# One stage of a hybrid layer with mixture of experts: the masking of the RWKV core's k products moves from VectorE to ScalarE and GpSimd

## What is computed

```python
def step(state, inp):
    r_t, w_t, k_t, v_t, kk_t, a_t = inp
    sa = jnp.einsum('bhij,bhj->bhi', state, -kk_t)
    state = (state * w_t[:, :, None, :]
             + sa[..., :, None] * (kk_t * a_t)[..., None, :]
             + v_t[..., :, None] * k_t[..., None, :])
    return state, jnp.einsum('bhij,bhj->bhi', state, r_t)
```

## Time and profile before

| | |
|---|---|
| median of 3 runs | 1987.44 us (1983.1 to 1991.18) |
| the profiled execution's own time | 1987.7 us |
| its span | 1986.1 us |
| TensorE matmul busy | 1891.4 us (95%) |
| TensorE weight loads busy | 1511.3 us (76%) |
| VectorE busy | 1577.8 us (79%) |
| ScalarE busy | 1212.9 us (61%) |
| GpSimd busy | 440.2 us (22%) |

### The profile page before, as it was taken

One profiled execution on the slowest core, in us unless ns is written; L12 is line 12 of the kernel. 1 busy time (PEld: TensorE's weight loads), 2 busy tenths in 40 slices (PEclk: granted clock), 3 DMA queues, 4 the chain that ended last, 5 costly groups with the idle time before them and its releaser, 6 DMA issues.

```text
span 1986.1 us, 27242 instructions
## 1 busy us (share of the span) xinstructions
PE 1891.4 (95%) x9408; PEld 1511.3 (76%) x9408; DVE 1577.8 (79%) x1614; ACT 1212.9 (61%) x1246; POOL 440.2 (22%) x385
## 2 busy tenths in 40 slices
PE   7999988999999889899999999999999999999997
PEld 5766655787767677788888888888888888888884
DVE  5763344775385569889999999999999999999996
ACT  5545564425374312467777777777777777777773
POOL 4535543001061421331111111111111111111110
PEclk9999998999999879799999999999999999999998
DMA  7535442414101124789999999999999999999993
GB/s 207 166 114 183 138 144 75 167 43 117 32 1 33 22 91 147 265 312 382 396 399 389 398 390 391 394 388 394 384 393 383 395 395 380 398 387 394 383 377 127
DMA packets 176497, 525.06 MB, mean 264 GB/s; under 512 B 30434, under 2 KB 47922, under 8 KB 176434
## 3 DMA queue, kind: packets, MB, share of 16 engines
q1 hardware_dynamic: 152722, 457.48, 60.2%
q0 software_dynamic: 21632, 66.74, 11.7%
q10 hardware_dynamic: 2080, 0.01, 0.1%
HBM read 499.06 MB, written 25.12 MB: 264 GB/s over the span
## 4 chain that ended last, share of the span: by engine, by line
PE 57%; DVE 2%; issue 0%; POOLq 0%; POOL 0%; DVEq 0%
PE banks L3436 53%; PE banks L3424 3%; PE banks L3430 1%; PE banks L3500 0%; DVE expert_weights L3774 0%; DVE x_tokens L3770 0%; PE banks L3521 0%; DVE weights_lo L3570 0%; DVE x_tokens L3781 0%; DVE x_tokens L3653 0%; PE banks L3557 0%; PE banks L3491 0%; DVE rows_lo L3600 0%; DVE member L3633 0%; DVE route_work L3675 0%
## 5 line engine op out<-in xcount | busy, mean ns | idle before, releaser
L3570 DVE TENSOR_TENSOR weights_lo<-expert_weights,weights_hi 128x2048 fp32r<-128x2048 f32 x384 | 877.1, 2288 | 65.6 <-ACT weights_hi L3810 61.3
L3810 ACT ACTIVATE weights_hi<-expert_weights 128x2048 fp32r<-128x2048 f32 x384 | 739.0, 1926 | 264.6 <-PE banks L3436 259.1
L3436 PE MATMUL banks<-weights_hi,rows_hi 128*128 128x512 f32 x1024 | 319.2, 393 | 0.0
L3436 PE MATMUL banks<-weights_hi,rows_lo 128*128 128x512 f32 x1024 | 315.5, 389 | 0.0
L3436 PE MATMUL banks<-weights_lo,rows_hi 128*128 128x512 f32 x1024 | 273.8, 389 | 0.0
L3436 PEld LDWEIGHTS banks<-weights_hi,rows_hi 128*128 128x128 f32 x1024 | 189.7, 188 | 44.9 <-issue 7.0
L3436 PEld LDWEIGHTS banks<-weights_hi,rows_lo 128*128 128x128 f32 x1024 | 192.2, 188 | 40.5
L3436 PEld LDWEIGHTS banks<-weights_lo,rows_hi 128*128 128x128 f32 x1024 | 192.2, 188 | 39.9
L3436 PE MATMUL banks<-weights_hi,u_hi 128*128 128x512 f32 x512 | 161.8, 397 | 0.0
L3436 PE MATMUL banks<-weights_hi,u_lo 128*128 128x512 f32 x512 | 158.8, 391 | 0.0
L3436 PE MATMUL banks<-weights_lo,u_hi 128*128 128x512 f32 x512 | 137.7, 391 | 0.0
(11 more groups left out here) (608 smaller groups left out, 2831.9 us busy)
## 6 DMA issues: line engine op xcount, KB each, us to landing
expert_weights<-in_exp_w SPq DMA_DIRECT2D x384, 1024.0 KB, 10.3
enter_rows<-in_ada_w POOLq DMA_DIRECT2D x24, 1024.0 KB, 5.7
w_in_landing<-in_w_in SPq DMA_DIRECT2D x16, 384.0 KB, 3.3
second_landing<-in_w_in SPq DMA_DIRECT2D x12, 512.0 KB, 4.0
x_tokens<-in_x SPq DMA_DIRECT2D x8, 512.0 KB, 7.1
w_in_landing<-in_w_in SPq DMA_DIRECT2D x8, 512.0 KB, 3.7
rwkv_room<-in_w_o SPq DMA_DIRECT2D x8, 512.0 KB, 7.5
w_in_landing<-in_w_in SPq DMA_DIRECT2D x12, 256.0 KB, 3.7
```

The lines of the kernel that those rows point to most:

```text
L3436: last = nc.tensor.matmul(c.banks[:, bank + n, :], left[:, 2 * q + kk, :], right[:, q, kk * FF + n * 512:kk * FF + (n + 1) * 512], start=s ...
L3570: nc.vector.tensor_tensor(w_lo[:, ch % SPLIT, :], c.raw[:, ch % RAW if place is None else place, :], w_hi[:, ch % SPLIT, :], ALU.subtract) ...
L3810: nc.scalar.activation(w_hi[:, ch % SPLIT, :], c.raw[:, ch % RAW if place is None else place, :], ACT.Copy).then_inc(hi_ready.sem, 1)
```

## The change

ScalarE copies both kinds of a unit's k products from PSUM into kv_mat as they are (copy_k), and GpSimd then zeroes what the mask zeroed, in place, with two affine selects. VectorE's mask function goes. kv_mat gets three slots. TensorE's k products of unit i wait for ScalarE's copy of unit i - 3, since that frees the banks; its mv units wait for GpSimd's selects. On ScalarE the copies of units 0 to 2 stand ahead of the 12 row copies, those of units 3 to 7 behind the square root of the latent sums, and the copies of banks 6 and 7 for tiles 0 and 1 stand behind copy_k(4) and copy_k(6).

```diff
--- before.py
+++ after.py
@@ -2632,7 +2632,8 @@
     X0 = work(TT, RH, P)
     bc_mat = work(TT, RH, P)
     staged = free(2, RH, P)
-    kv_mat = Carve(X0.rearrange("p t h s -> p (t h s)"))(2, 2, 4, P)
+    KV = 3
+    kv_mat = Carve(X0.rearrange("p t h s -> p (t h s)"))(KV, 2, 4, P)
     scale = Carve(staged.rearrange("p a h s -> p (a h s)"))
     scale_next, rhs = scale(TT - 1, RP, P), scale(RW)
     state = free(TT - 1, RP, P)
@@ -2649,6 +2650,7 @@
     rows_turned, rows_copied = own("token_rows_turned"), own("token_rows_copied")
     latent_sums, latent_roots, latent_ready = own("latent_sums"), own("latent_roots"), own("latent_ready")
     k_ready, k_masked, mv_done, mv_copied = own("k_products_ready"), own("k_products_masked"), own("mv_done"), own("mv_copied")
+    k_copied = own("k_products_copied")
     y_ready, y_copied, x_ready, x_taken = own("y_ready"), own("y_copied"), own("x_ready"), own("x_taken")
     z_ready, z_copied, j_ready, j_copied = own("z_ready"), own("z_copied"), own("join_ready"), own("join_copied")
     scales, rhs_ready, rhs_added, u_ready, u_copied = (own("scales_ready"), own("rhs_ready"), own("rhs_added"), own("u_ready"),
@@ -2722,6 +2724,15 @@
                 nc.gpsimd.memset(XTB[:].rearrange("p a b -> p (a b)")[:, 0:S * S:S + 1], 1.0).then_inc(cleared.sem, 1)
                 nc.gpsimd.memset(inverse, 0.0).then_inc(x_cleared.sem, 1)
 
+                for i in range(units):
+
+                    pool.wait_ge(k_copied.sem, i + 1)
+                    for kind, compare in enumerate((ALU.is_gt, ALU.is_ge)):
+                        place = kv_mat[:, i % KV, kind]
+                        last = nc.gpsimd.affine_select(out=place, in_=place, compare_op=compare, fill=0.0, base=0,
+                                                       pattern=[[0, 4], [1, P]], channel_multiplier=-1)
+                    last.then_inc(k_masked.sem, 1)
+
                 pool.wait_ge(solved.sem, 1)
                 for t in range(TT - 1):
                     along = lambda x, at: x[:, :, at:at + 1].broadcast_to([P, RP, P])
@@ -2779,7 +2790,7 @@
                             pe.wait_ge(b_masked.sem, 5 + i)
                         else:
 
-                            pe.wait_ge(k_masked.sem, i - 2)
+                            pe.wait_ge(k_copied.sem, i - 2)
                         for h, f, j, n in heads_of(q):
                             both = ar[rows_of(j), f, t, :, :].rearrange("p k s -> p (k s)")
                             last = nc.tensor.matmul(c.banks[:, 2 * (i % 3) + j, (n // 2) * 2 * P:(n // 2 + 1) * 2 * P],
@@ -2800,8 +2811,8 @@
                             pe.wait_ge(mv_copied.sem, t)
                         for h, f, j, n in heads_of(q):
                             v = v_tok[:, t, h * 64:(h + 1) * 64]
-                            nc.tensor.matmul(c.banks[:, 6, h * 64:(h + 1) * 64], kv_mat[:, g % 2, 0, n, :], v, start=True, stop=True)
-                            last = nc.tensor.matmul(c.banks[:, 7, h * 64:(h + 1) * 64], kv_mat[:, g % 2, 1, n, :], v,
+                            nc.tensor.matmul(c.banks[:, 6, h * 64:(h + 1) * 64], kv_mat[:, g % KV, 0, n, :], v, start=True, stop=True)
+                            last = nc.tensor.matmul(c.banks[:, 7, h * 64:(h + 1) * 64], kv_mat[:, g % KV, 1, n, :], v,
                                                     start=True, stop=True)
                         last.then_inc(mv_done.sem, 1)
 
@@ -2949,6 +2960,20 @@
                     pair = c.banks[:, 2 * (i % 4):2 * (i % 4) + 2, :].rearrange("p j (m k s) -> p m j k s", m=2, k=2)
                     nc.scalar.activation(by_pair(staged[:, t % 2, 4 * q:4 * q + 4, :]), pair[:, :, :, 0, :], ACT.Copy).then_inc(b_raw.sem, 1)
 
+                def copy_k(i):
+
+                    act.wait_ge(k_ready.sem, i + 1)
+                    if i >= KV:
+
+                        act.wait_ge(mv_done.sem, i - KV + 1)
+                    pair = c.banks[:, 2 * (i % 3):2 * (i % 3) + 2, :].rearrange("p j (m k s) -> p m j k s", m=2, k=2)
+                    for kind in range(2):
+                        last = nc.scalar.activation(by_pair(kv_mat[:, i % KV, kind]), pair[:, :, :, kind, :], ACT.Copy)
+                    last.then_inc(k_copied.sem, 1)
+
+                act.wait_ge(latent_sums.sem, 1)
+                for i in range(KV):
+                    copy_k(i)
                 for n in range(3 * TT):
                     dst, t = (v_tok, b_tok, k_tok)[n // TT], n % TT
 
@@ -2969,7 +2994,11 @@
                     act.wait_ge(variances.sem, t + 1 + more)
                     nc.scalar.activation(r_head[:, t, heads], s_head[:, t, heads], ACT.Sqrt).then_inc(roots.sem, 1)
 
-                for t in range(TT):
+                for i in range(KV, units):
+                    copy_k(i)
+                    if i % 2 == 0:
+                        mv(i // 2 - 2)
+                for t in range(TT - 2, TT):
                     mv(t)
                 for t in range(TT):
 
@@ -3037,18 +3066,6 @@
                     nc.vector.tensor_tensor(by_pair(bc_mat[:, t, 4 * q:4 * q + 4, :]), pair[:, :, :, 1, :], four(c.upper[:]),
                                             ALU.mult).then_inc(b_masked.sem, 1)
 
-                def mask(i):
-
-                    dve.wait_ge(k_ready.sem, i + 1)
-                    if i >= 2:
-
-                        dve.wait_ge(mv_done.sem, i - 1)
-                    pair = c.banks[:, 2 * (i % 3):2 * (i % 3) + 2, :].rearrange("p j (m k s) -> p m j k s", m=2, k=2)
-                    nc.vector.tensor_tensor(by_pair(kv_mat[:, i % 2, 0]), pair[:, :, :, 0, :], four(c.upper_strict[:]), ALU.mult)
-                    nc.vector.tensor_tensor(by_pair(kv_mat[:, i % 2, 1]), pair[:, :, :, 1, :], four(c.upper[:]), ALU.mult).then_inc(k_masked.sem, 1)
-
-                for i in range(2):
-                    mask(i)
                 dve.wait_ge(cleared.sem, 1)
                 dve.wait_ge(blocks_in.sem, 16)
                 for i in range(S - 1):
@@ -3062,8 +3079,6 @@
                         c.dve(dve, last)
                     else:
                         last.then_inc(solved.sem, 1)
-                    if i % 3 == 2 and i < 18:
-                        mask(2 + i // 3)
                     if i == 20:
                         dve.wait_ge(latent_roots.sem, 1)
                         nc.vector.reciprocal(latent["roots"], latent["roots"]).then_inc(latent_ready.sem, 1)
```

## The result

The changed kernel takes 1988.92 us (median of 19 runs, 1985.74 to 1993.78), the kernel before 1984.37 (19 runs, 1979.41 to 1991.18). The ratio is 1.0027 with a 95% interval of 1.0020 to 1.0034: slower by 4.0 to 6.7 us. The forecast was 1.2 us faster; the time lies inside the range that I gave, on the side of rival 2.

A forecast was written before the change was run, and what follows sets the result against it. VectorE's solving was taken as the bound, moving to the ScalarE and TensorE chain. Transposes 0.65 us earlier and 0.59 us of DMA wait gone gave -1.2 us: 1986.5 us, or 1986.3 against the median; range 1979.5 to 1996.

The forecast's parts named there:

- rival 2: TensorE's clock falls in a new stand: +3 us if ahead of mv4, +8 us if ahead of mv2; chance 0.30.
- What bounds the kernel before: VectorE's solving ends last and releases TensorE's gate products; every microsecond gained or lost there passes on one for one.
- What the change removes: Masks leave VectorE: six inside the solving free 11.3 us, the two outside it are worth nothing.
- A select's time: On GpSimd, a select over 512 columns takes 0.63 us; the other bound was 1.27 to 1.73 us.
- What a select costs the solving: Each GpSimd select holds VectorE's solving up by about 0.5 us; ten cost 5.0 us (bounds 0 and 12.7).
- ScalarE's queue: Mv bank copies wait behind copy_k(4): mv unit 2 starts 2.6 us later, 0.4 first delay and 2.2 queueing.
- At the low clock for the last two units, as now: TensorE's mv chain ends 7.12 us after mv6 starts at 661.85, so at 669.0.
- second form: TensorE's clock falls ahead of mv2, slowing mv2, mv3, k5 and k6 too: +8 us, about 1995.5.
- The wait for the inverses' DMA: Block inverses reach SBUF 5 us earlier, so the 0.59 us wait for their DMA at 677.35 goes.
- Rival 1: TensorE's clock stays at 1.00 throughout: -4.4 to -7.0 us, about 1982; chance 0.20.

The follow-up runs named there:

- The filled kernel before: Kernel before, with the last k unit's products repeated once in the stand ahead of mv unit 6: 1983.57 us, ratio 1.0006.
- the swapped kernel: Changed kernel with ScalarE's copies of banks 6 and 7 for tiles 0 and 1 ahead of the k copies of units 4 and 6: 1974.92 us, ratio 0.9963.
- its repeat: The named kernel run once more, unaltered, for a second profile: kernel before 1984.05 us, changed kernel 1987.5 us.
- the one without selects: Changed kernel without GpSimd's selects for units 3 to 7 (ten of sixteen), those k products left unmasked: 1989.05 us, ratio 1.0036.
- the kernel before with slower copies: Kernel before, with about 2 us of delay in ScalarE's copies of banks 6 and 7 for tiles 0 and 1: 1991.61 us, ratio 1.0052.
- the filled kernel: Changed kernel, with TensorE repeating the next k unit's products twice in the stands ahead of mv units 2 and 4: 1976.99 us, ratio 0.9975.
- the swapped one without selects: Changed kernel with mv copies ahead of the k copies and no GpSimd selects for units 3 to 7: 1974.51 us, ratio 0.9955.

## Why the prediction was wrong

- **What bounds the kernel before: right.** The filled kernel before shows it. That the bound would move to the chain over ScalarE and TensorE was right too: the gate products follow the last mv unit, over 16 us after the solving has ended.
- **What the change removes: right.** Without any select the solving takes 23.4 us; 34.81 - 11.3 gave 23.5. The masks ahead of the solving were worth nothing: it started 16.6 us after the core's start before and 16.9 after.
- **A select's time: right.** 0.63 was taken, the median is 0.637.
- **What a select costs the solving: too high.** 0.5 us each was taken, 5.0 in all. Measured: 2.8 us for the eight that fell into the solving in the changed kernel (the last unit's came after its end), 3.2 for the ten of the swapped one, so 0.32 to 0.35 each. A lengthened instruction takes 0.3 to 0.4 us more, which is less than a select. The strict form of the rule in the Trainium skill (SBUF — State Buffer, "Who interferes with whom"), by which one of the two is blocked for the whole instruction of the other, would have made it a whole select each. The trace agrees that the two slow each other, and not with that price: within the 1.39 us of the pair of selects from 642.05 (a pair takes 1.23 at 666.49, beside no VectorE instruction) VectorE ran an addition to its end and most of a product. The prediction's "So the two engines exclude each other" was taken from one select, L617, and is more than this trace bears out.
- **ScalarE's queue: right.** Mv unit 2 was forecast 2.6 us later and came 2.3 later (28.8 against 26.5 from the core's start), with a stand of 2.63 against the forecast 2.4.
- **The step that failed** is the one behind "At the low clock for the last two units, as now". It took over the place of the clock's fall from the trace before, while the same section lengthened the stands ahead of it from 0.57 to 2.4 us. The stands were 2.46 to 2.63 us, and the clock fell in the first of them or within 0.4 us of its end in all four profiles that have one (the changed kernel, its repeat, the one without selects, the kernel before with slower copies). In none of the eight profiles with short or filled stands did it fall before the stand ahead of mv unit 6. That was rival 2 in its second form, with its terms nearly right: 1.7 us more for an mv unit (1.6 taken), 0.95 for a k unit (1.0), the gate products at 59.7 from the core's start (rival 2: 673.2 + 5.2 = 678.4, which is 60.3). The transposes came 7.0 later than before, not 8: the clock rose within the gate products, and from the first of them to the first transpose it was 4.9 us, not 6.1.
- **The wait for the inverses' DMA: mis-sized.** 0.59 us was to be gained at the second transposes. They start 1.43 us after the first (683.34 - 681.91), where it was 1.66, so 0.2 was gained; a wait of 0.39 for ScalarE's copy stands there instead.
- **What is left over.** The 5.4 us of the ratio and the 7.0 of the profiles differ. The core's remainder behind the first transposes takes between 62.9 and 67.0 us in the twelve profiles, with a second stretch at the low clock that lies elsewhere each time. What moves it was not tried.
- **The chances.** Rival 2 had 0.30 and the forecast 0.40. The page of the Trainium skill on TensorE (TensorE: Matmul & The Clock Gate, "Why this matters for your kernels"), which speaks of idle gaps as what brings the clock down, was cited for rival 2 and given no weight against the forecast. The page has longer gaps in view than the stands here, and gives nothing for short ones. The runs agree with its direction: 1.9 us of repeated matmuls in each of the two stands gave back nearly 10 us on the chain.
- **Rival 1** is what the swapped kernel became, without the queueing that rival 1 had: gate products released by the solving at 43.6, the transposes by the inverses, and 7.3 us gained where rival 1 had 4.4 to 7.0.

What stays open: what decides where the clock falls around a stand of 1.4 us. Five profiles have such a stand ahead of mv unit 6 with the clock at 1.00. It fell in the stand in two (the kernel before and its repeat), 2.4 us after the stand in two (the filled kernel, the swapped one without selects), and not there in one (the swapped kernel).

## What to carry to other kernels

When a copy is handed to another engine, look at what it is queued ahead of: a copy for which someone waits, whose input is ready, must not stand behind a copy whose input is still to come. When a change lengthens TensorE's idle stretches, don't take the place of the clock's fall from the trace before; cost both, or fill the stretch. And give a stand two prices, its own length and the clock behind it: here the queueing with the clock up left a kernel about 5 us faster than the one before (0.9975), and with the clock down one 5 us slower (1.0027).

## What was not expected of the hardware

- 3.8 us of matmuls that nobody reads, put into two stands, made the kernel about 10 us faster (ratio 0.9975 where it was 1.0027), because the clock stayed at 1.00 for some 17 us longer.
- A select of 0.64 us on GpSimd beside a product or an addition of 0.41 us on VectorE, both on SBUF, lengthens VectorE's instruction by only some 0.35 us, and the pair of selects by 0.16 (1.39 against 1.23).
